# The first RMS norm of a three-block fp32 kernel: its gain loaded in two pieces behind the input, root and gain applied in one operation, nine warming products instead of sixteen

## The reference

```python
def rms_norm(x, gain):
    xf = x.astype(jnp.float32)
    y = xf * lax.rsqrt(jnp.mean(xf * xf, axis=-1, keepdims=True) + RMS_EPS)
    return (y * gain.astype(jnp.float32)).astype(x.dtype)

hn = rms_norm(h, gains[0])          # h = x, the input
proj = hn @ w_in                    # first projection of the attention
```

## Time and profile before

| | us |
|---|---|
| median of 3 runs | 1185.75 |
| lowest, highest | 1184.82, 1187.96 |
| the profiled execution | 1185.63 |
| its span | 1183.8 |
| TensorE busy in the span | 1159.6 (98%) |
| VectorE busy | 845.8 (71%) |
| ScalarE busy | 651.8 (55%) |
| GpSimd busy | 142.3 (12%) |

### The profile page before, as it was taken

One profiled execution on the slowest core, in us unless ns is written; L12 is line 12 of the kernel. 1 busy time (PEld: TensorE's weight loads), 2 busy tenths in 40 slices (PEclk: granted clock), 3 DMA queues, 4 the chain that ended last, 5 costly groups with the idle time before them and its releaser, 6 DMA issues.

```text
span 1183.8 us, 23069 instructions
## 1 busy us (share of the span) xinstructions
PE 1159.6 (98%) x9804; PEld 1067.9 (90%) x9804; DVE 845.8 (71%) x1297; ACT 651.8 (55%) x1171; POOL 142.3 (12%) x145
## 2 busy tenths in 40 slices
PE   8999999999999999999999999999999999999998
PEld 8897789999889898978999988999989878999986
DVE  6677778888648988887788875866577776655642
ACT  4647656666537665745666663565535434644530
POOL 1320000000003232100000000112433410000000
PEclk9999999999999999999999999999999999999999
DMA  8832235565635453354655564542332323655440
GB/s 307 274 143 90 89 131 199 189 214 183 248 107 172 161 193 125 116 190 158 249 186 193 192 249 162 189 169 107 109 108 73 128 89 128 247 214 190 173 172 36
DMA packets 31766, 196.80 MB, mean 166 GB/s; under 512 B 4016, under 2 KB 5680, under 8 KB 9520
## 3 DMA queue, kind: packets, MB, share of 16 engines
q1 hardware_dynamic: 27504, 185.04, 43.7%
q10 hardware_dynamic: 4160, 10.29, 2.7%
HBM read 193.22 MB, written 1.05 MB: 164 GB/s over the span
## 4 chain that ended last, share of the span: by engine, by line
PE 89%; DVE 7%; ACT 2%; issue 2%; DMA 1%; POOL 0%; DVEq 0%; POOLq 0%; ACTq 0%; SPq 0%
PE bank L573 24%; PE bank L575 24%; PE bank L574 23%; DVE wlo L562 2%; PE bank L1195 1%; PE bank L1252 1%; PE bank L775 1%; PE bank L1279 1%; PE bank L1966 1%; DVE xc L1666 1%; PE bank L2559 1%; PE bank L2616 1%; PE bank L2574 1%; PE bank L807 1%; PE bank L2570 1%
## 5 line engine op out<-in xcount | busy, mean ns | idle before, releaser
L562 DVE TENSOR_TENSOR wlo<-raw,whi 128x1024 fp32r<-128x1024 f32 x322 | 387.5, 1244 | 54.7 <-ACT whi L554 54.3
L573 PE MATMUL bank<-xT,wlo 128*128 128x256 f32 x1488 | 417.2, 280 | 2.5 <-DVE xc L1666 1.4
L575 PE MATMUL bank<-xT,whi 128*128 128x256 f32 x1488 | 411.7, 277 | 0.0
L574 PE MATMUL bank<-xT,whi 128*128 128x256 f32 x1488 | 411.7, 277 | 0.0
L554 ACT ACTIVATE whi<-raw 128x1024 fp32r<-128x1024 f32 (+1 forms) x349 | 348.6, 1050 | 66.4 <-PE bank L575 32.9
L573 PEld LDWEIGHTS bank<-xT,wlo 128*128 128x128 f32 x1488 | 279.4, 188 | 5.6 <-DVE xc L1666 1.9
L574 PEld LDWEIGHTS bank<-xT,whi 128*128 128x128 f32 x1488 | 279.5, 188 | 0.6 <-issue 0.5
L575 PEld LDWEIGHTS bank<-xT,whi 128*128 128x128 f32 x1488 | 279.3, 188 | 0.0
L712 POOL TENSOR_TENSOR rr<-rr,nhalf 128x1 f32<-128x1 f32 x34 | 21.0, 618 | 700.0 <-DVE rr L700 516.6
L575 PE MATMUL bank<-whi,gT 128*128 128x512 f32 x264 | 103.9, 394 | 0.0
L574 PE MATMUL bank<-wlo,gT 128*128 128x512 f32 x264 | 103.3, 391 | 0.0
(11 more groups left out here) (400 smaller groups left out, 1826.4 us busy)
## 6 DMA issues: line engine op xcount, KB each, us to landing
raw<-in_wall SPq DMA_DIRECT2D x173, 1024.0 KB, 4.9
grow<-in_rows ACTq DMA_DIRECT2D x13, 512.0 KB, 5.3
h<-in_x SPq DMA_DIRECT2D x4, 256.0 KB, 5.3
grow<-in_rows ACTq DMA_DIRECT2D x4, 256.0 KB, 3.2
memx<-in_mem ACTq DMA_DIRECT2D x1, 1024.0 KB, 9.4
out<-h SPq DMA_DIRECT2D x4, 256.0 KB, 2.0
D<-Tx ACTq DMA_DIRECT2D x4, 128.0 KB, 6.0
D<-Tx ACTq DMA_DIRECT2D x4, 127.5 KB, 6.4
```

Of the source, the lines that this page charges most:

```text
L562: e.tensor_tensor(low, src, high, SUB).then_inc(*up("dve.low", p))
L573: e.matmul(out, a[1], b[0], start=start, stop=False)
L574: e.matmul(out, a[0], b[1], start=False, stop=False)
L575: return e.matmul(out, a[0], b[0], start=False, stop=stop)
```

## The change

1. The gain of the first norm is no longer issued by ScalarE as one load of 512 KB but by SyncE as two of 256 KB, after the four pieces of the input and ahead of the first chunks, with semaphores of their own (`first0`, `first1`).
2. VectorE's multiplication by the gain and its scaling by the root become one operation, `dve_first_norm` (input × root × gain). It now waits for the root. The small addition of the sums stands ahead of it, and the second tile's between the first tile's halves.
3. On ScalarE and VectorE the first half chunk is no longer handled between the two tiles' copies of the transposed rows but behind both.
4. TensorE does nine warming products ahead of the transposes instead of sixteen; the eight behind them stay.
5. The load of the next norm's gain into the same buffer waits for the new operation's last event.

The new operation is written with the same arithmetic up to the order of two multiplications.

```diff
--- before.py
+++ after.py
@@ -741,6 +741,13 @@
                 e.wait_ge(*at("pe.norm", *turned))
             e.tensor_tensor(halves(xs_of(k, t))[n], halves(src)[n], grow2[:, 512 * n:512 * n + 512], MUL).then_inc(
                 *up("dve.norm", "y", k, t, n))
+
+        def dve_first_norm(e, t, n):
+            e.wait_ge(*at(f"h{t}{n}"))
+            e.wait_ge(*at(f"first{n}"))
+            e.wait_ge(*at("pool.norm", "sum", 0, t))
+            e.scalar_tensor_tensor(halves(xs_of(0, t))[n], halves(h[:, t, :])[n], rr[:, 2 * t + 1:2 * t + 2],
+                                   halves(grow2)[n], MUL, MUL).then_inc(*up("dve.norm", "xs", 0, t, n))
 
         def dve_norm_scale(e, k, t):
             e.wait_ge(*at("pool.norm", "sum", k, t))
@@ -2903,6 +2910,9 @@
                 for n in range(2):
                     e.dma_start(h[:, t, 512 * n:512 * n + 512], x_d[128 * t:128 * t + 128, 512 * n:512 * n + 512]).then_inc(
                         *up(f"h{t}{n}", by=16))
+            for n in range(2):
+                e.dma_start(grow2[:, 512 * n:512 * n + 512], rowsrc("g_nsa", 512 * n, 512)).then_inc(
+                    *up(f"first{n}", by=16))
             for i in range(NRAW):
                 sp_load(e, i)
             e.dma_start(cols[:, :], cols_d).then_inc(*up("cols", by=16))
@@ -2922,19 +2932,17 @@
         def scalar(e):
             split = Split(lambda p: act_high(e, p), ENDS)
             e.dma_start(ident, masks_d[:, 0:128]).then_inc(*up("ident", by=16))
-            act_gain(e, 1, "g_nsa")
             e.wait_ge(*at("pool.const", "nhalf"))
             e.activation(rr[:, 0:1], nhalf[:, :], ACTF.Square).then_inc(*up("act.const", "table"))
             for t in range(2):
                 act_norm_sums(e, 0, t, h[:, t, :], [(f"h{t}{n}",) for n in range(2)])
-            act_norm_high(e, 0, 0)
-            split.one()
-            act_norm_high(e, 0, 1)
+            for t in range(2):
+                act_norm_high(e, 0, t)
             split.to(2)
             act_nsa_in(e, split)
             e.wait_ge(*at("dve.const", "gon"))
             e.wait_ge(*at("srow", "galog"))
-            e.wait_ge(*at("dve.norm", "y", 0, 1, 1))
+            e.wait_ge(*at("dve.norm", "xs", 0, 1, 1))
             act_gain(e, 1, "g_ffn0")
             walk(NSA_ORDER["act"], {"s": scoring(nothing, lambda n: act_exp(e, n)),
                              "t": turning(nothing, lambda n: act_turned(e, n)),
@@ -2989,15 +2997,14 @@
         def vector(e):
             split = Split(lambda p: dve_low(e, p), ENDS)
             e.wait_ge(*at("act.const", "table"))
-            for t in range(2):
-                for n in range(2):
-                    dve_norm_gain(e, 0, t, n, h[:, t, :], "g_nsa", [(f"h{t}{n}",) for n in range(2)])
-                dve_norm_sums(e, 0, t)
-            for t in range(2):
-                dve_norm_scale(e, 0, t)
-            dve_norm_low(e, 0, 0)
-            split.one()
-            dve_norm_low(e, 0, 1)
+            dve_norm_sums(e, 0, 0)
+            dve_first_norm(e, 0, 0)
+            dve_norm_sums(e, 0, 1)
+            dve_first_norm(e, 0, 1)
+            dve_first_norm(e, 1, 0)
+            dve_first_norm(e, 1, 1)
+            for t in range(2):
+                dve_norm_low(e, 0, t)
             split.to(2)
             e.wait_ge(*at("negf"))
             e.tensor_copy(negb[:, :], negf[:, 0:negf_w - 1]).then_inc(*up("dve.const", "negb"))
@@ -3080,7 +3087,7 @@
             split = Split(lambda p: None, ENDS)
             e.wait_ge(*at("ident"))
 
-            for _ in range(16):
+            for _ in range(9):
                 e.matmul(banks[0][:, 0:128], ident, ident, start=True, stop=True)
             for t in range(2):
                 pe_norm_turn(e, 0, t)
```

## The result

| | before, us | after, us |
|---|---|---|
| median of 20 runs | 1185.21 | 1187.23 |
| lowest, highest | 1184.53, 1187.96 | 1185.77, 1189.92 |
| the profiled execution | 1185.63 | 1186.99 |
| its span | 1183.8 | 1185.2 |

The ratio is 1.0018 with a 95% interval from 1.0012 to 1.0024: the changed kernel is 1.4 to 2.8 us slower. The forecast was 1.8 us faster, so the sign is wrong.

The account below looks back on a forecast made before the run. TensorE was taken to bound the kernel (busy 98% of the span). Line 1077 starting 1.8 us earlier gave 1185.63 − 1.8 = 1183.8 us; forecast case 1182.9 to 1185.0 (0.60), overall range 1182.2 to 1186.8.

Parts of the forecast that it names:

- the gain's landing: First norm: the gain's two halves follow the input on SyncE at 0.75 us each and land at 6.9 and 7.6.
- The upper bound, 8.3: Latest landing of both gain halves: issued at about 3, plus the lone gain transfer's 5.3 us for 512 KB.
- The first chunk lands when it did: Weight transfers at the front: over 8:10 the engines are full, so bytes decide, not issues, and the first chunk is no later.
- some hundredths: TensorE around the transposes: it never stands still for more than a few hundredths of a us.
- first rival: Gain pieces land late behind 1 MB of input; gain nil with the second at 9.8: 1185.6; 0.17 including a late clock rise.
- late clock rise: TensorE's pace doubles later than 10.1; a rise at 13.6 costs 1.75 us; chance 0.17 together with late gain pieces.
- forecast start of 14.7: TensorE's first product with a low part, line 1077, starts at 14.7 instead of 16.52, 1.8 us earlier.
- All that only eats slack: Later weight chunks: lateness, up to 0.7 us for chunk 2, stays hidden; TensorE multiplies the fourth chunk from about 32 on.
- third rival: Shift given back later: the weight stream sets the pace at the first softmax, so the end hardly moves: 1185.3; chance 0.09.
- the same bytes stand ahead of them as before: Weight transfers: issued 0.9 us later behind two more DMAs, but the bytes ahead are unchanged, the gain's 512 KB formerly in another queue.
- move along: Behind the scores at 51.19: softmax, splitting and the DMA at 459.47 shift with their releases, so the 1.8 us last.
- second rival: A pause before the transposes keeps the clock low: rise at 13.6 gives 1185.6, later is slower, 1187.3 at 17 (chance 0.06).

Follow-up runs that it names:

- own rows: Changed kernel with the gain read from 128 copies in memory, one row per partition; 1186.25 against 1185.84, ratio 1.0003.
- only the move: Kernel before with only the first norm's gain loaded by SyncE in two pieces behind the input; 1188.09 against 1185.85, ratio 1.0020.
- one piece: Changed kernel with the gain in one 512 KB load on SyncE's queue, same place behind the input; 1186.31 against 1185.84, ratio 1.0006.
- masks later: Changed kernel with the 452 KB mask load behind the fifth chunk instead of ahead of the fourth; 1186.16 against 1185.85, ratio 1.0003.

## Why the prediction was wrong

Right were: the squares (forecast 3.9, 4.6, 5.4, 6.2; measured 3.74, 4.45, 5.60, 6.22); the joined operation at 0.75; eighteen warming records that end about 8; the first root in time (sum at 5.28, GpSimd's operation from 5.64 for 0.55, so ready at 6.2 instead of 6.6); and that nobody waits for the first three chunks, since ScalarE works through six half chunks without a wait from 13.85.

**The step that failed first is the gain's landing.** "I take 0.75 a piece as what 256 KB of this shape cost with nothing beside them", and from it 6.9 and 7.6 for the two halves. Measured, 8.8 and 9.8: issued at 2.58 and 3.04, to landing 6.2 and 6.8 us. The upper bound, 8.3, was wrong too, since the lone gain transfer of before (5.3 us from its issue) ran from an almost empty start, not behind 1 MB. Rows from other loads were carried over to a broadcast behind a full megabyte, and the broadcast moved fewer bytes a microsecond (277 GB/s over 6 to 8 us). "The first chunk lands when it did" fell with it: it landed at 12.4 (issued at 3.5, 8.9 us), before at 10.6 (2.6 and 8.0). The operations then ended at 12.04 instead of 10.25 and TensorE paused for 1.55 us, which the forecast put at some hundredths. The first rival had this mechanism and its price, "The gain is nil with it at 9.8", and measured was a second piece at 9.8 and line 1084 at 16.95 against 16.36: nil, and 0.6 worse. It had a chance only together with a late clock rise, 0.17, and it stopped at nil: no case of late pieces was worked out in which the kernel gets slower. With the gain out of the queue and no pause the forecast start of 14.7 came true in one profile (14.68; 15.40 and 16.73 in the versions with one product, which pause).

**The second is that slack was asserted, not measured.** "All that only eats slack: TensorE multiplies the fourth chunk from about 32 on." TensorE did not wait for the fourth chunk. It waited at 40.04 for the fifth, because ScalarE and VectorE take a chunk only in their own list's order: behind the fourth chunk stand VectorE's copy `Tx` (line 1140), ScalarE's four DMA issues behind it (2.7 us), the small piece, a second `Tx` with its four issues (2.8 us), and only then the fifth. From the landing to TensorE that is 40.04 − 24.93 = 15.1 us of chain. The wait of 3.02 us of before was off the chain, as the prediction says under its third rival, but not by much: the chunk had landed at 22.08, and with 24.93 it costs 0.9 us. So TensorE's need was met by a landing up to 24.0, in before, 0.6 us ahead, up to 23.4: a slack of 1.4 us where the text counted ten. The same sum from the other four kernels in which TensorE waited (sixteen products, own rows, only the move, before with nine; waits of 1.4, 2.2, 1.7 and 0.4) gives 1.0, 0.5, 0.7 and 0.9. In the kernel in which TensorE spreads the gain, with four products, line 1084 starts 1.7 us ahead of before, the chunk lands at 22.0 and nothing waits, which asks for 1.6 at least. So by this estimate, from one execution each, the slack was about a microsecond, 0.5 to somewhat over 1.6. The forecast also took the lateness of that chunk as unchanged ("the same bytes stand ahead of them as before"). The bytes are the same, the landing isn't:

| | fourth chunk issued | landed |
|---|---|---|
| before | 17.03 | 22.1 |
| after | 17.39 | 24.9 |
| after, sixteen products | 17.34 | 25.0 |
| gain from own rows | 16.28 | 24.2 |
| only the move | 18.56 | 26.0 |
| one piece on SyncE | 18.22 | 23.9 |
| masks later | 18.10 | 23.8 |
| gain on ScalarE's queue, nine; sixteen | 17.05; 16.56 | 22.0; 22.4 |
| before with nine products | 16.55 | 22.9 |
| gain by TensorE, one; four | 15.90; 15.12 | 20.8; 22.0 |
| gain by TensorE, masks later | 15.86 | 20.6 |
| gain behind the first tile's squares | 22.72 | 28.9 |

All four kernels with two gain pieces in SyncE's queue and the masks ahead of the fourth chunk have it at 24.2 or later, 7.4 to 8.0 us behind its issue. All others have it 4.8 to 6.9 us behind, and those without a gain in that queue have it by 22.9, save the last row, whose chunk is issued 5 us later. Without a gain in the queue the figure alone moves between 4.8 and 6.9, so one row by itself proves little. The third rival (given back by the weight stream ahead of the first softmax) was half the truth, with 0.09.

Together, by the profiled executions: line 1084 is 0.6 us later, TensorE waits 0.9 for `wlo` at 40, and the scores follow a gap of 1.63 us (the chain's "issue"); in before the waits list names one of 0.7. These come to 2.4; measured are 2.2 at the scores (53.42 less 51.19). The shift is as large at VectorE's same work at 385.47 against 383.31, but 1.7 at the DMA of the earlier trace rows (461.15 against 459.47) and 1.4 at the end of the span. Between 380 and 400 TensorE of before waits 0.6 us for a `wlo`, and that of after doesn't. So the shift did not simply "move along", as the forecast had it.

The medians differ by 2.0, not 1.4. Here the granted clock comes in. Its mean over the execution was 0.996 in seven of the twenty of after, which took 1188.20 to 1189.92 us; the other thirteen have a median of 1186.99, still above the highest median of before, 1185.85. Of the 92 executions of before beside the experiments two had 0.996. So the loss is there without these executions, and they add the last tenths. Whether the change or the occasion brought them is not shown: with sixteen products none of eleven had it.

**The pause and the clock.** The second rival, a pause that keeps the clock low, was half right. After the pause all sixteen transposes ran at the slow pace (3.62 us; 1.91 in the same view of before), so the clock rose some 3 us later. It cost nothing that shows here, since the run with sixteen products had the fast pace and the same start of line 1084. In the kernels with one gain load on ScalarE's queue and nine products, with one piece, and with the masks later, a granted clock near 0.5 followed pauses of 1 to 2.7 us. The Trainium skill, "TensorE: Matmul & The Clock Gate", section "HAM oscillation — how this bites in real kernels", says that a wait for data between bursts of products, if it is long enough, brings the clock down, so that the next burst starts slow. These three traces agree (0.50 to 0.55 over 12 to 14 us), though their waits are shorter than those that the page describes. With the gain from own rows, with the move alone and with nine products alone, pauses of 0.7 to 2.7 us had no such fall behind them, so how often it happens is not settled by one profile each. In before with nine products a pause of 1.9 us left line 1077 at 15.89, 0.5 us earlier than with sixteen.

**What stays open.** Why the queue falls behind. The trace's single records show that of the sixteen DMA engines the first had finished its part of the first gain piece at 6.2 and the last two at 8.6 and 8.8; of the fourth chunk one finished its part at 24.9, the others between 21.7 and 23.0. In before the parts of that chunk ended between 21.4 and 22.1. A transfer has landed when its last part has. Whether the reads of one shared row put that engine behind is not shown: with own rows the fourth chunk is late too. Open also is the 0.9 us that the gap ahead of the scores grew by: in all other kernels but one it is 0.73 again, with sixteen products too, so it may belong to the one execution. And open is how the 2.0 to 2.5 us of the spread gain come about, as said there: fewer bytes, an earlier front and no broadcast were changed together.

## What to carry to other kernels

A load placed behind others in a full queue landed here with the slowest engine's share, so bound such a load by a row from the same queue at the same load, not by bytes at the peak rate; and a small vector that every partition needs may be cheaper loaded once and spread by a product on an idle TensorE than read 128 times (here 2.0 to 2.5 us faster than before). Before a late transfer is called hidden, follow the list of the engine that takes it to the next thing that somebody waits for: the slack is what is left at the end of that list, not the time until the chunk itself is multiplied. Joining two operations brought nothing here, since the first of them had been running in a wait.

## What the runs showed of the hardware

The same 512 KB broadcast took 5.3 to 5.7 us from its issue when issued first beside the input, 6.9 behind it in one queue, and 9.2 when issued at 4.53 on a second queue beside loads already under way. Reading it from 128 rows instead of one saved 0.9 us for the first half and 1.2 for the second; the DMA engines were about equally busy over 6 to 8 us (1.01 and 1.06) and moved 277 and 407 GB/s. An operation with a scalar and a tensor took 0.75 us whether its tensor came from `grow` or from a bank. The granted clock fell to half once in some executions in the middle of the kernel, as at 404 us above, without anything the change touches near it. And the column of the granted clock says 1.00 in the first microseconds, where the pace of TensorE's records is half that of later ones.
